# The passes of the feed-forward part on TensorE: copies written out, or a loop

## The chip, the cores and the metric

The kernel runs on one core of a Trainium2 chip. The metric is the device time of one execution in microseconds (us). Three runs of the kernel before are given, and their median counts.

## The reference, cut to what matters

One layer of a decoder trunk, for 512 tokens of width 2048 in float32: a mixer sub-layer and a feed-forward sub-layer, each with a residual. The change lies in the second:

```
hf = modulate(rms_norm(x, norm_ffn_gain), sh_f, sc_f)
gate_h, up_h = split(hf @ w_ffn_in, 2)          # (512, 2048) @ (2048, 11264)
x = x + g_f * ((silu(gate_h) * up_h) @ w_ffn_out)   # (512, 5632) @ (5632, 2048)
```

## The kernel before

Each engine has a program of its own, written out in order in one function, and they meet only at semaphores. The hidden width of 5632 is worked in FG = 11 groups of 512. For each group the two input products (gate and up) are made as two jobs each, a job being a product by a 2 x 2 Winograd scheme: seven block products instead of eight. Every float32 product is made of three passes in a reduced format, high by high, low by high and high by low parts. Two rounds make a job (one for each half of the contraction), so that a group has eight rounds. A round (`wino_round`, lines 1116 to 1141) has seven blocks of 4 x 3 = 12 matmuls of 256 columns. The product with `w_ffn_out` is made by `down_tile`: 16 tiles of 4 x 3 = 12 matmuls of 512 columns in a group.

The rounds overlap the groups: the first eight rounds stand ahead, then come FG - 1 = 10 passes (lines 1162 to 1180), each with rounds 0 and 1 of line 1165, the 16 down tiles of the group before, a matmul without use at line 1175, and rounds 2 to 7. After the passes the last group's down tiles follow.

What the matmuls need is made elsewhere. SyncE loads pairs of weight blocks into the buffer `raw` (line 457), ScalarE writes their high parts `fhi` (lines 1486 and 1496), VectorE makes sums of blocks and most low parts `flo` (lines 2074 to 2092), drains PSUM (lines 2118 to 2126) and adds the down products to the residual (line 2245), GpSimd makes the other low parts (lines 616 and 626). These four already run the passes as hardware loops: lines 486, 630, 1561 and 2249 are `with <engine>.Fori(0, ...) as j`. TensorE's passes are a Python loop that writes out ten copies.

Before each block TensorE waits for its low part, `low_pool` or `low_dve`; before each down tile for `low_pool` and `y_added` (lines 1169 and 1170), before the first also for `drained` and `h_lo` (line 1172); before some rounds for `drained` (line 1144) or `y_added` (line 1125). In a pass these are 97 waits. The values waited for come from the class `Round`, whose methods return a constant when j is a Python number and an expression of a register when j is a loop variable:

```
def ahead(self, n, per):
    return n if self.j is None else per * self.j + n
def blocks(self, n):
    return self.ahead(self.block + n, 72)
def lows(self, n):
    return self.ahead(self.low + n, 32)
def owns(self, n):
    return self.ahead(self.own + n, 40)
```

The buffers and PSUM banks that a pass uses do not depend on j: a pass moves the ring of six blocks by 72 and the buffer of eight by 48 places.

Of the kernel before, what the change touches and what calls it, by code (L numbers as in the profile page):

```python
# [20 lines left out]
FG = FFN // (4 * P)  # L21
# [51 lines left out]
def layer_kernel(nc, xt, wstream, mstream, vecs, rows, tabs, cmp_tab, up, pool_w, w1, w2, out):  # L73
    with ExitStack() as ctx:
# [568 lines left out]
        def _(pe):  # L643
# [472 lines left out]
            def wino_round(at, job, half, slot, entry=False, banks=None):  # L1116

                for i in range(7):
                    s = at.ring(i)
                    if i in POOL_LOWS:  # L1120
                        pe.wait_ge(low_pool, at.lows(POOL_LOWS.index(i) + 1))
                    else:
                        pe.wait_ge(low_dve, at.owns(DVE_LOWS.index(i) + 1))
                    if banks is not None and i in banks:
                        pe.wait_ge(*banks[i])
                    c = COMBO[i]
                    if entry and 2 <= i < 6:
                        pe.wait_ge(t_low, 4 * half + i - 1)
                    if entry and i == 6:
                        pe.wait_ge(b_low, 8 * (half + 1))  # L1130
                    bank, side = PLACE[i]
                    acc = ps[:, 4 * slot + bank, side * HALF:(side + 1) * HALF]
                    for kp in range(4):
                        if entry and i < 2:
                            pe.wait_ge(b_low, 8 * half + 2 * kp + i + 1)
                        w = slice(kp * P, (kp + 1) * P)
                        for n, (wo, xo) in enumerate(((fhi, hfH), (fhi, hfL), (flo, hfH))):
                            ins = nc.tensor.matmul(acc, wo[:, s, w], xo[half][:, c, kp, :],  # L1138
                                                   start=half == 0 and side == 0 and kp == 0 and n == 0,
                                                   stop=half == 1 and kp == 3 and n == 2, skip_group_check=True)  # L1140
                    ins.then_inc(blk_used, 1)

            def free_slot(job):
                pe.wait_ge(drained, job)

            def down_tile(at, d, bank, kk):
                s = at.ring(d)
                for k in kk:
                    col = slice(k * P, (k + 1) * P)
                    ins = passes(ps[:, bank, :], huH[:, k, :], huL[:, k, :], fhi[:, s, col], flo[:, s, col],  # L1150
                                 False, k == 0, k == 3)
                return ins
# [5 lines left out]
            for x in range(4, 8):  # L1158
                if x % 2 == 0:
                    free_slot(x // 2 - 1)  # L1160
                wino_round(Round(x), x // 2, x % 2, x // 2 % 2)
            for j in range(FG - 1):
                free_slot(4 * j + 3)
                for x in range(2):
                    wino_round(Round(x, j), 0, x, 0)
                at = Down(j)
                pe.wait_ge(drained, 4 * j + 4)
                for d in range(KD):
                    pe.wait_ge(low_pool, at.lows(d + 1))
                    pe.wait_ge(y_added, 16 * j + (d + 1))  # L1170
                    if d == 0:
                        pe.wait_ge(h_lo, 2 * j + 2)
                    down_tile(at, d, 4 + d % 4, range(4)).then_inc(blk_used, 1)
                pe.wait_ge(drained, 4 * j + 5)
                nc.tensor.matmul(ps[:, 1, 0:P], ident[:, :], ones[:, :], start=True, stop=True)
                for x in range(2, 8):
                    if x in (4, 6):
                        free_slot(4 * j + x // 2 + 3)
                    wino_round(Round(x, j), x // 2, x % 2, x // 2 % 2, banks=None if x != 2 else {
                        0: (y_added, 16 * j + 17), 1: (y_added, 16 * j + 18), 2: (y_added, 16 * j + 20)})  # L1180
# [1225 lines left out]
```

## Time and profile before

| | |
|---|---|
| median of three runs | 2467.75 us (2460.15 to 2467.84) |
| profiled execution | 2467.75 us, span 2466.0 us |
| mean granted TensorE clock over the span | 0.972 of 2.4 GHz |
| TensorE busy | 96% of the span, 14,813 matmuls and as many weight loads |
| VectorE, ScalarE, GpSimd busy | 65%, 39%, 41% |
| ten passes | from about 1167 to 2417 us |

In the rows, PE is TensorE's matmuls and PEld its weight loads, DVE is VectorE, ACT ScalarE, POOL GpSimd and SP SyncE; a q behind the name (PEldq) marks what the sequencer handles alone. L1138 is line 1138 of the kernel. The span is the profiled time from the first to the last instruction, and times in the rows count from its start. PEclk is the granted share of 2.4 GHz. EVENT_SEMAPHORE is a separate wait, ALU_OP and FUSED_REGOPS are register operations, COMPARE_BRANCH is a loop's branch. Queues of the kind "instruction" bring program code.

### The profile page before, as it was taken

The numbers are of one execution on the slowest core, as the hardware profiler recorded it, in microseconds if no ns is written. First come the engines' busy times: TensorE is split into PE (matmuls) and PEld (weight loads), VectorE is DVE, ScalarE is ACT, GpSimd is POOL, SyncE is SP. The second block draws the span as 40 slices with busy tenths as digits, with TensorE's granted clock in tenths as the row PEclk, the third lists the DMA queues.
The fourth block names the chain that finished last, engine by engine and source line by source line (L and its number), as shares of the span: only waits on it lengthen the run. The fifth ranks groups of instructions, "written<-read, shape, count | busy, mean of one in ns | idle before, by whom it ended". The sixth has DMA issues, their size and how long they took to land.

```text
span 2466.0 us, 40619 instructions
## 1 busy us (share of the span) xinstructions
PE 2377.2 (96%) x14813; PEld 2121.7 (86%) x14813; DVE 1610.9 (65%) x2449; ACT 971.7 (39%) x1804; POOL 1014.8 (41%) x782
## 2 busy tenths in 40 slices
PE   7989999999799999969999999999999999999999
PEld 5867777877699888859898989898989898999997
DVE  6746335466788577698485858585857575757573
ACT  5343223333566522245343434343434343434332
POOL 5853333446577544312424242424242424242423
PEclk7899999999799999979999999999999999999999
DMA  9842134566112377513333232323232323232323
GB/s 368 284 160 74 60 103 156 185 217 231 47 61 68 129 251 254 196 35 103 103 103 103 103 103 99 107 88 118 86 120 86 120 86 120 86 116 90 111 87 128
DMA packets 86300, 317.16 MB, mean 129 GB/s; under 512 B 9585, under 2 KB 10241, under 8 KB 84737
## 3 DMA queue, kind: packets, MB, share of 16 engines
q1 hardware_dynamic: 84240, 303.31, 36.3%
q10 hardware_dynamic: 1904, 11.62, 1.2%
q8 instruction: 118, 1.93, 0.3%
q14 instruction: 38, 0.30, 0.0%
HBM read 310.69 MB, written 4.19 MB: 128 GB/s over the span
## 4 chain that ended last, share of the span: by engine, by line
PE 75%; issue 11%; DVE 6%; POOL 5%; DMA 1%; ACT 0%; SPq 0%; POOLq 0%; ACTq 0%; DVEq 0%
PE ps L1138 35%; PE ps L647 31%; POOL wlo L513 5%; PE ps L1030 2%; PE ps L1019 1%; PE ps L986 1%; PE ps L987 1%; PE ps L719 1%; DVE macc L1603 1%; DMA modx<-in_mstream 1%; DVE pacc L1628 1%; DVE biasT L1950 0%; PE ps L1085 0%; DVE hf L2159 0%; POOL pacc L534 0%
## 5 line engine op out<-in xcount | busy, mean ns | idle before, releaser
L1138 PE MATMUL ps<-hfH,fhi 128*128 128x256 f32 x2464 | 710.6, 288 | 23.5 <-DVE hfL L2178 7.5
L1138 PE MATMUL ps<-hfH,flo 128*128 128x256 f32 x2464 | 700.9, 284 | 0.0
L1138 PE MATMUL ps<-hfL,fhi 128*128 128x256 f32 x2464 | 693.9, 282 | 0.0
L616 POOL TENSOR_TENSOR flo<-raw,fhi 128x512 fp32r<-128x512 f32 x176 | 241.6, 1373 | 784.2 <-ACT fhi L1486 783.8
L1138 PEld LDWEIGHTS ps<-hfH,fhi 128*128 128x128 f32 x2464 | 466.6, 189 | 26.9 <-issue 12.9
L1138 PEld LDWEIGHTS ps<-hfL,fhi 128*128 128x128 f32 x2464 | 478.6, 194 | 0.0
L1138 PEld LDWEIGHTS ps<-hfH,flo 128*128 128x128 f32 x2464 | 465.0, 189 | 0.0
L1486 ACT ACTIVATE fhi<-fsum 128x512 fp32r<-128x512 f32 x352 | 221.0, 632 | 392.6 <-DVE fsum L2074 130.9
L2092 DVE TENSOR_TENSOR flo<-fsum,fhi 128x512 fp32r<-128x512 f32 x352 | 307.9, 887 | 9.5
L2245 DVE SCALAR_TENSOR_TENSOR x1T<-ps,modc,x1T 128x512 f32<-128x512 f32 x176 | 132.1, 751 | 273.5 <-PE ps L647 270.8
L626 POOL TENSOR_TENSOR flo<-raw,fhi 128x512 fp32r<-128x512 f32 x176 | 234.4, 1345 | 155.6 <-ACT fhi L1496 154.9
L647 PE MATMUL ps<-huH,fhi 128*128 128x512 f32 x704 | 275.8, 392 | 1.2 <-DVE huL L2135 1.2
L647 PE MATMUL ps<-huH,flo 128*128 128x512 f32 x704 | 276.7, 393 | 0.0
L647 PE MATMUL ps<-huL,fhi 128*128 128x512 f32 x704 | 275.7, 392 | 0.0
L513 POOL TENSOR_TENSOR wlo<-raw,whi 128x512 fp32r<-128x512 f32 x112 | 158.5, 1417 | 250.1 <-ACT whi L1277 250.1
L1496 ACT ACTIVATE fhi<-raw 128x512 fp32r<-128x512 f32 x176 | 109.0, 630 | 255.8 <-PE ps L647 206.8
L520 POOL TENSOR_TENSOR wlo<-raw,whi 128x512 fp32r<-128x512 f32 x100 | 144.9, 1459 | 150.0 <-ACT whi L1207 143.7
L1486 ACT ACTIVATE fhi<-raw 128x512 fp32r<-128x512 f32 x264 | 163.4, 624 | 86.0 <-PE ps L647 49.1
L647 PE MATMUL ps<-whi,hmH 128*128 128x512 f32 x448 | 185.4, 414 | 5.5 <-DVE xs L1822 2.9
L1603 DVE SCALAR_TENSOR_TENSOR macc<-modw,cact,macc 128x512 f32<-128x512 f32 x165 | 183.2, 1110 | 7.0 <-DMA modw<-in_mstream 1.4
L1277 ACT ACTIVATE whi<-raw 128x512 fp32r<-128x512 f32 x120 | 75.4, 630 | 264.3 <-PE ps L647 263.7
L647 PE MATMUL ps<-wlo,hmH 128*128 128x512 f32 x448 | 178.7, 399 | 0.0
(321 smaller groups left out, 4226.7 us busy)
## 6 DMA issues: line engine op xcount, KB each, us to landing
raw<-in_wstream SPq DMA_DIRECT2D x370, 512.0 KB, 4.1
modw<-in_mstream SPq DMA_DIRECT2D x144, 512.0 KB, 5.4
modx<-in_mstream SPq DMA_DIRECT2D x32, 512.0 KB, 5.5
modg<-in_mstream SPq DMA_DIRECT2D x16, 512.0 KB, 5.4
xT<-in_xt SPq DMA_DIRECT2D x4, 1024.0 KB, 8.1
w1s<-in_w ACTq DMA_DIRECT2D x2, 2048.0 KB, 8.8
x1T<-in_xt ACTq DMA_DIRECT2D x4, 1024.0 KB, 8.2
out_y<-x1T SPq DMA_DIRECT2D x16, 256.0 KB, 2.0
```

The lines of the kernel that those rows point to most:

```text
L513: nc.gpsimd.tensor_tensor(wlo[:, s, :], raw[:, r, :], whi[:, s, :].bitcast(F32), ALU.subtract).then_inc(unit_ready, 1)
L520: TT(wlo[:, u % SPLIT, :], raw[:, u % 8, :], whi[:, u % SPLIT, :].bitcast(F32), ALU.subtract).then_inc(unit_ready, 1)
L616: TT(flo[:, s, :], src, fhi[:, s, :].bitcast(F32), ALU.subtract).then_inc(low_pool, 1)
L626: TT(flo[:, s, :], raw[:, at.slot(d), :], fhi[:, s, :].bitcast(F32), ALU.subtract).then_inc(low_pool, 1)
L647: ins = nc.tensor.matmul(acc, lhs, rhs, start=first and n == 0, stop=last and n == 2)
L1138: ins = nc.tensor.matmul(acc, wo[:, s, w], xo[half][:, c, kp, :], start=half == 0 and side == 0 and kp == 0 and n == 0, stop=half == 1 and ...
L1277: A(whi[:, u % SPLIT, :], raw[:, u % 8, :], ACT.Copy).then_inc(unit_hi, 1)
L1486: A(fhi[:, at.ring(i), :], src, ACT.Copy).then_inc(blk_hi, 1)
L1496: A(fhi[:, at.ring(d), :], raw[:, at.slot(d), :], ACT.Copy).then_inc(blk_hi, 1)
L1603: ins = V.scalar_tensor_tensor(out=macc[:, :], in0=src, scalar=scal, in1=macc[:, :], op0=ALU.mult, op1=ALU.add)
L2092: V.tensor_tensor(flo[:, s, :], src, fhi[:, s, :].bitcast(F32), ALU.subtract).then_inc(low_dve, 1)
L2245: V.scalar_tensor_tensor(out=x1T[:, d, :], in0=ps[:, bank, :], scalar=modc[:, M_GF + d:M_GF + d + 1], in1=x1T[:, d, :], op0=ALU.mult, op1= ...
```

## The change

TensorE's ten passes become a hardware loop of its own. The body is the same; the values of its waits become expressions of the loop's register. Nothing else is changed, on TensorE or elsewhere.

```
-            for j in range(FG - 1):
+            with pe.Fori(0, FG - 1) as j:
                 free_slot(4 * j + 3)
                 for x in range(2):
                     wino_round(Round(x, j), 0, x, 0)
```

## Rows read from the trace of the kernel before

**Rows 1.** The page: busy time of TensorE, and the chain that ended last.

```profile
PE 2377.2 (96%) x14813; PEld 2121.7 (86%) x14813; DVE 1610.9 (65%) x2449; ACT 971.7 (39%) x1804; POOL 1014.8 (41%) x782
...
PE ps L1138 35%; PE ps L647 31%; POOL wlo L513 5%; PE ps L1030 2%; PE ps L1019 1%; PE ps L986 1%; PE ps L987 1%; PE ps L719 1%; DVE macc L1603 1%; DMA modx<-in_mstream 1%; DVE pacc L1628 1%; DVE biasT L1950 0%; PE ps L1085 0%; DVE hf L2159 0%; POOL pacc L534 0%
```

**Rows 2.** Stretches of 125 us: busy us and count of each engine.

```profile
core 0: us, PE busy (x) PEld busy (x) DVE busy (x) ACT busy (x) POOL busy (x), PEclk, DMA share, GB/s
1231.10:1356.10 125.00, 125.00 (x868) 116.86 (x867) 82.28 (x120) 49.05 (x80) 43.01 (x32) 1.00 0.31 102
...
2231.10:2356.10 125.00, 125.00 (x868) 116.86 (x867) 82.29 (x120) 49.06 (x80) 43.04 (x32) 1.00 0.31 102
```

**Rows 3.** Line 1175: count, duration in ns, first and last start in us.

```profile
L1175 PE MATMUL ps<-ones,ident x20: 270/272/273, 1231.1 to 2356.3; 128*128 128x128 f32 x20
```

**Rows 4.** Instruction queue q8 (packets, MB, share): pass 1481.1 to 1606.1; whole run.

```profile
q8 instruction: 7, 0.11, 0.4%
...
q8 instruction: 118, 1.93, 0.3%
```

**Rows 5.** Register work of the loops on VectorE and ScalarE, ten passes: ns min/median/max.

```profile
L2249 DVEq FUSED_REGOPS  x10: 62/63/63, 1159.8 to 2285.2; - x10
L370 ACTq ALU_OP  x390: 35/35/49, 1159.8 to 2407.3; - x195
L370 DVEq ALU_OP  x170: 40/40/52, 1161.9 to 2407.3; - x170
L2087 DVEq ALU_OP  x390: 40/40/40, 1164.1 to 2409.2; - x195
L2089 DVEq ALU_OP  x160: 40/40/40, 1165.7 to 2408.5; - x160
```

**Rows 6.** Lines 1172 and 647 from 1558 to 1563 us.

```profile
L1172 PEldq EVENT_SEMAPHORE  x1: 51/51/51, 1559.9 to 1559.9; - x1
...
L647 PEld LDWEIGHTS ps<-huH,fhi x2: 187/187/187, 1561.8 to 1562.4; 128*128 128x128 f32 x2
```

**Rows 7.** VectorE's loop, line 2249: a taken branch, then the last.

```profile
L2249 DVEq ALU_OP  x1: 40/40/40, 1409.7 to 1409.7; - x1
L2249 DVEq COMPARE_BRANCH  x1: 67/67/67, 1409.8 to 1409.8; - x1
L2249 DVEq FUSED_REGOPS  x1: 63/63/63, 1410.1 to 1410.1; - x1
...
L2249 DVEq COMPARE_BRANCH  x1: 50/50/50, 2409.9 to 2409.9; - x1
```

**Rows 8.** Instruction queues: 1159 to 1285; 1300 to 2410 (no q14); 2411.1 to 2412.

```profile
q14 instruction: 3, 0.02, 0.1%
...
q8 instruction: 61, 1.00, 0.4%
...
q14 instruction: 1, 0.01, 3.8%
```

**Rows 9.** DMA issues of the run: count, KB each, median us to landing.

```profile
raw<-in_wstream SPq DMA_DIRECT2D x370, 512.0 KB, 4.1
...
ident<-in_tabs SPq DMA_DIRECT2D x1, 64.0 KB, 2.1
```

**Rows 10.** TensorE's waits near 548, 402, 2423 us, and stretches just after them.

```profile
PE ps L647 <- POOL wlo L513: 2.6, 1, 2.6
...
PE ps L647 <- DVE xs L1822: 2.9, 2, 2.1
...
PE ps L647 <- DVE huL L2135: 1.2, 1, 1.2
...
404.20:407.60 3.40, 2.90 (x7) 2.35 (x8) 3.37 (x14) 0.00 (x0) 0.00 (x0) 0.50 0.00 0
...
551.00:554.40 3.40, 3.40 (x9) 2.64 (x8) 3.33 (x3) 0.14 (x1) 3.40 (x3) 0.51 0.36 133
...
2424.00:2431.00 7.00, 7.00 (x31) 5.72 (x32) 3.00 (x4) 2.54 (x4) 4.48 (x4) 1.00 0.14 36
```

More of the change, by code:

```diff
@@ L1161, in _ @@
                 wino_round(Round(x), x // 2, x % 2, x // 2 % 2)
-            for j in range(FG - 1):
+            with pe.Fori(0, FG - 1) as j:
                 free_slot(4 * j + 3)
```

## The prediction

> **What bounds the kernel now.** I read the page first, then the stretches of the feed-forward part, the one instruction that occurs once in a pass, the instruction transfers, and last the loops that other engines already run. The page says that TensorE is busy 96% of the span and heads the chain of work that ended last, with line 1138 (the Winograd rounds) as its largest entry [rows 1]. The stretches say more: between 1231 and 2356 us TensorE is busy 125.00 us of 125.00, at a granted clock of 1.00 (2.4 GHz) in the first pass as in the last, while DVE has 82, ACT 49 and POOL 43 us of work [rows 2]. So in these ten passes TensorE waits for nobody, and every us that it stops is a us on the end. The pass itself: the warming matmul of line 1175 stands once in it (two records each, 0.1 us apart), first at 1231.1 and last at 2356.3 us [rows 3], so one pass takes (2356.3 - 0.1 - 1231.1) / 9 = 125.0 us.
>
> How its code arrives is the second thing to see. In one pass TensorE runs 868 + 867 recorded matmuls and weight loads [rows 2] and some twenty separate waits (1755 instructions), and queue q8 brings 7 instruction packets, 0.11 MB [rows 4]: packets of 16 KB with about 1755 / 7 = 250 instructions each, one every 18 us. Over the run q8 brought 118 packets, 1.93 MB [rows 4]. That is straight code that streams in; none of it stops TensorE today.
>
> **What the change removes and adds.** It removes nine of ten copies of the pass from TensorE's program. The matmuls, weight loads, waits and signals executed are the same in number and order: 84 matmuls in each of eight rounds, 192 in the down tiles, one for warmth. Nothing moves between engines, and no other queue changes. It adds four things.
>
> *Register work for the waits.* A wait for 72j + 56 was a constant and is now computed. The other engines show the price: for DVE one operation of 40 ns before most waits, for ACT 35 ns, and once a pass a fused operation of some 60 ns [rows 5]. TensorE has 97 waits in a pass, of which no two neighbours share a value, so some 97 x 0.04 + 5 x 0.06 = 4.2 us of sequencer work a pass. It lies ahead of the array: the wait of line 1172 (before the first down tile) was dealt with at 1559.9 us, and the first weight load of that tile starts at 1561.8 us [rows 6]. So the sequencer runs 1.9 to 2.0 us ahead (some 17 matmuls of 0.12 us), with one or two register operations per block of 12 matmuls (12 x 0.12 = 1.44 us). Cost 0; if that cover were gone, 4.2 x 10 = 42 us.
>
> *The loop's own instructions.* On DVE the add (40 ns), the compare-and-branch and then the first instruction of the next pass stand at 1409.7, 1409.8 and 1410.1 us [rows 7]: 0.3 us from branch to next instruction, though the target is there. With the first register operations 0.45 us per taken branch. Under a lead of 2.0 us it costs nothing by itself.
>
> *Code that must be there when the branch is taken.* The body is 1755 + about 105 = 1860 instructions, 1860 / 250 = 7.4 packets of 16 KB, so it touches 8 blocks, perhaps 9, and the block after it is fetched ahead. The nearest row is DVE's loop: q14 (8 KB packets) brought 3 in the stretch of its first pass, and from 1300 to 2410 us none at all [rows 8], so its body is kept. But that body is 120 busy instructions [rows 2] and, of three lines alone, (170 + 390 + 160) / 10 = 72 register operations [rows 5]: at some 128 instructions to an 8 KB packet it touches two or three blocks, not eight. No row says that a body of TensorE's length is kept. I take it that the first block has been overwritten when the branch comes, so that it is fetched anew at each of the 9 taken branches.
>
> The price of that fetch, F, has to be bounded. When DVE left its loop (branch at 2409.9 us, rows 7), q14 was empty up to 2411.1 and then had one packet [rows 8]: over 1.2 us from need to start. A 16 KB packet then takes 0.3% of 16 engines' 2466 us over 118 packets, 118 / 118 = 1.0 us [rows 4]. Low end 2.2 us. High end: 4.1 us, the landing of a 512 KB weight transfer among others [rows 9]. Between them: a 64 KB transfer lands in 2.1 us [rows 9], of which a 4 KB share of one engine is a small part; with 1.0 us for the packet 2.9, and some more for the weight loads that keep the queues 30% busy [rows 2]. I take 3.3.
>
> The stall per branch is then 0.45 + 3.3 - 2.0 = 1.75 us (0.65 at the low end, 2.55 at the high), and nine make 16 us.
>
> *The clock.* After a stop the granted clock may fall to half (1.2 GHz). A wait of 2.6 us near 548 us was followed by 3.4 us at 0.51; one of 2.1 us near 402 by 3.4 us at 0.50; one of 1.2 us near 2423 left it at 1.00 [rows 10]. A stop of 1.75 lies between. Where the clock falls, the array does half the work for 3.4 us, so 1.7 us are lost, in nine such places 15 us, or twice that if it stays down twice as long. I take it as kept for the likeliest case.
>
> **A rule against this.** The row above gives a lead of 2.0 us. The Trainium skill, "Advanced Engine Details and Errata", section "Engine Queue Depths", gives TensorE's queue 64 entries. By that, 32 matmuls of 0.12 us, 3.8 us, would be queued when the branch is reached, 0.45 + 3.3 would be covered, and the sum would be 0. The trace's lead speaks against it. The skill's "Runtime: NRT & Kernel Launch", section "Instruction fetch mechanics", speaks both ways: 2048 instructions of room for PE, which would hold 1860, and a fetch stall for a taken branch outside a two-page window. No run here shows either yet.
>
> **Sum.** The profiled execution took 2467.75 us with a span of 2466.0, and is itself the median of the three runs. 2467.75 + 9 x 1.75 = 2483.5 us, +0.6%. A measurement of this kernel tells about 0.3% (7.4 us) from no change.
>
> **Rivals.**
> 1. *The code stays, or the lead covers the fetch* (the side of no change). For it: DVE's, ACT's and POOL's loops run without a fetch, and the body is a sixteenth of the 118 packets. Against it: length, and a measured lead of 2.0 us against a need of at least 2.65. It decides where 0.45 + F falls under 2.0 + 0.8. Time: 2467.75 plus nine branches that cost nothing, 2468 us. Were F at its low end, 9 x 0.65 = 6 us, 2474, still inside 0.3%. Chance 0.28.
> 2. *The clock falls too.* A stop of over 2 us at every back edge, 1.7 to 3.4 us more for each: 9 x (1.75 + 1.7) = 31 to 9 x (2.55 + 3.4) = 54 us, 2499 to 2521. For it: two waits of 2.1 and 2.6 us did it. Against it: the rest of each 125 us is dense. Chance 0.24.
> 3. *Register work comes out into the open*: if a wait on a register value keeps the sequencer from running ahead, up to 42 us, 2510. Against it: no DVE row shows its wait instructions slow. Chance 0.05.
> 4. *Faster.* There is no wait in these passes to take away; only fewer instruction packets (0.4% of the DMA share in a pass). Chance 0.02, some 2460.
>
> **How the numbers follow.** The likeliest (one fetch per branch, clock kept) has 0.41, with its own range 2474 to 2492 (F from 2.2 to 4.1, stops of 0.65 to 2.55: 6 to 23 us). The range has to reach down to rival 1, whose chance is too large to leave out, and up into rival 2: 2465 to 2508, leaving out the upper part of rivals 2 and 3 and most of rival 4. Slower by over 0.3% means over 2475.2: 0.39 of the likeliest, 0.24 and 0.05, together 0.68. Same: 0.28 and 0.02, 0.30. Faster 0.02.
>
> **What would show it.** Right: a gap of 1 to 2.5 us before the first matmul of line 1138 at nine places 126 to 127 us apart, put down to issue and not to a semaphore; q8 with one or two packets a pass; the rest of the pass 125.0 us as before; register operations on the weight loads' sequencer with no gap behind them. Wrong for want of a fetch: no q8 packet in the later passes and no gap. Wrong in size: a stretch at 0.5 clock behind the gaps, or more than one gap a pass. Seven q8 packets a pass would mean that nothing is kept; the sum stays, since blocks further on are fetched ahead.

## The result, and the profile after

The loop is slower. Over four runs each, the median is 2506.65 us (2504.11 to 2509.25) against 2463.95 us for the kernel before: 42.7 us more, a ratio of 1.0175 with a 95% interval of 1.0147 to 1.0202. The forecast was 2483.5 us, 16 us more. The way and the range held, and the size was less than half of what came.

The profile of the changed kernel, first the page, in the lines that answer to [rows 1] and to the whole run in [rows 4]:

```profile
span 2510.2 us, 41370 instructions
...
PE 2389.8 (95%) x14813; PEld 2130.7 (85%) x14813; DVE 1621.4 (65%) x2449; ACT 973.6 (39%) x1804; POOL 1014.4 (40%) x782
...
q8 instruction: 137, 2.24, 0.4%
...
issue 43%; PE 30%; POOL 20%; DVE 7%; DMA 1%; ACT 1%; POOLq 0%; ACTq 0%; DVEq 0%; SPq 0%
```

As many matmuls as before. The chain that ended last runs through "issue" for 43% of the span, where it was 11% in the kernel before; that share is no measure of the loss, since TensorE's stops in the loop add up to 29 of 2510 us (below). The code queue brings 137 packets, more than the 118 of the straight program, though nine of the ten copies of the pass are gone: 9 packets come in each pass.

Next, line 1175, once a pass as in [rows 3], and the loop's own instructions at line 1162 (count, ns min/median/max, first and last start):

```profile
L1175 PE MATMUL ps<-ones,ident x20: 270/272/273, 1233.1 to 2399.3; 128*128 128x128 f32 x20
...
L1162 PEldq FUSED_REGOPS  x10: 50/50/53, 1166.8 to 2332.5; - x10
L1162 PEldq ALU_OP  x10: 32/32/32, 1291.7 to 2456.7; - x10
L1162 PEldq COMPARE_BRANCH  x10: 76/5282/5727, 1291.8 to 2456.8; - x10
```

A pass takes (2399.3 - 0.1 - 1233.1) / 9 = 129.6 us instead of 125.0. The last branch, not taken, takes 76 ns, and a taken one 5.3 us in the median; DVE's took 67 ns and 0.3 us to the next instruction [rows 7]. The stall arises there.

One of the nine branches in order of time: the instruction itself, the matmuls around it, and stretches with the granted clock, as in [rows 2].

```profile
L1162 PEldq COMPARE_BRANCH  x1: 5514/5514/5514, 1549.1 to 1549.1; - x1
L1162 PEldq FUSED_REGOPS  x1: 50/50/50, 1554.6 to 1554.6; - x1
```

```profile
1550.95 0.28 PE L1138 MATMUL ps<-hfH,flo 128*128 128x256 f32 x1
1554.85 0.58 PE L1138 MATMUL ps<-hfH,fhi 128*128 128x256 f32 x1 [3.61 <-issue]
1555.22 0.41 PE L1138 MATMUL ps<-hfL,fhi 128*128 128x256 f32 x1
```

```profile
1549.00:1551.20 2.20, 2.20 (x19) 2.02 (x18) 2.07 (x4) 1.44 (x3) 0.00 (x0) 1.00 0.89 296
1551.20:1554.80 3.60, 0.03 (x1) 0.00 (x0) 0.49 (x1) 1.21 (x3) 1.26 (x1) 0.78 0.29 115
1554.80:1560.00 5.20, 5.15 (x24) 5.16 (x25) 2.16 (x4) 0.63 (x1) 0.00 (x0) 0.50 0.01 3
1560.00:1566.00 6.00, 6.00 (x53) 6.00 (x53) 5.80 (x12) 3.28 (x5) 1.29 (x1) 1.00 0.52 175
```

The branch begins at 1549.1 us. Until 1551.2 the array works off what was queued, 2.1 us, the lead of [rows 6]. Then it stands for 3.6 us, and when it starts again its clock is at 0.50 (1.2 GHz) up to 1560. In those 5.2 us it does half the work, so 2.6 us more are lost.

What TensorE waited for in the loop (total us, times, longest):

```profile
PE ps L1138 <- issue: 18.1, 5, 3.8
PE ps L1138 <- POOL flo L616: 11.1, 4, 3.2
```

### The profile page after: what moved, and what is told of

Same layout as the page of the kernel before. It is cut to its first block, busy times and chain, and to the rows that moved or that the text cites. A ratio compares the mean times of both kernels' runs of the same rounds, so it can differ in the third digit from the quotient of the medians.

```text
span 2510.2 us, 41370 instructions
## 1 busy us (share of the span) xinstructions
PE 2389.8 (95%) x14813; PEld 2130.7 (85%) x14813; DVE 1621.4 (65%) x2449; ACT 973.6 (39%) x1804; POOL 1014.4 (40%) x782
## 4 chain that ended last, share of the span: by engine, by line
issue 43%; PE 30%; POOL 20%; DVE 7%; DMA 1%; ACT 1%; POOLq 0%; ACTq 0%; DVEq 0%; SPq 0%
PE ps L647 15%; POOL flo L616 7%; POOL flo L626 7%; PE ps L1138 6%; POOL wlo L513 5%; PE ps L1030 2%; PE ps L1019 1%; PE ps L986 1%; PE ps L719 1%; PE ps L987 1%; PE ps L740 1%; DVE macc L1603 1%; DVE pacc L1628 1%; DVE biasT L1950 0%; PE ps L1085 0%
## 5 line engine op out<-in xcount | busy, mean ns | idle before, releaser
L1138 PE MATMUL ps<-hfL,fhi 128*128 128x256 f32 x2464 | 702.4, 285 | 0.0
L1138 PEld LDWEIGHTS ps<-hfH,fhi 128*128 128x128 f32 x2464 | 476.5, 193 | 58.1 <-issue 32.1
L1138 PEld LDWEIGHTS ps<-hfH,flo 128*128 128x128 f32 x2464 | 473.9, 192 | 0.0
L2092 DVE TENSOR_TENSOR flo<-fsum,fhi 128x512 fp32r<-128x512 f32 x352 | 321.7, 927 | 10.1
L647 PE MATMUL ps<-whi,hmL 128*128 128x512 f32 x448 | 178.8, 399 | 0.0
```

What stands on the lines that cost most here:

```text
L647: ins = nc.tensor.matmul(acc, lhs, rhs, start=first and n == 0, stop=last and n == 2)
L2092: V.tensor_tensor(flo[:, s, :], src, fhi[:, s, :].bitcast(F32), ALU.subtract).then_inc(low_dve, 1)
```

## The experiments

Each run is compared with runs of the kernel before on the same chip; "loop" is the changed kernel.

**1. The register work alone.** Ten copies as before, with the waits on a register that is counted up between them:

```
-            for j in range(FG - 1):
+            j_reg = pe.alloc_register("pass_j")
+            pe.reg_mov(j_reg, 0)
+            for copy in range(FG - 1):
+                j = pe.snap(j_reg, min_val=0, max_val=FG - 2)
 ...
+                pe.reg_add(j_reg, j_reg, 1)
```

> Ten passes written out, but every wait of a pass is on a register value as in the loop; no branch. Theory (the branch waits for code): the register work hides under the sequencer's lead, 2464 us as the kernel before, within 5, no gap at the pass ends. Rival (register work or waits on register values slow TensorE): 2500 to 2510 us as the loop. Both in part: between, say 2475.

2467.09 us against 2465.56; ratio 1.0007 (0.9992 to 1.0023). TensorE's register operations stand in its trace at 32 ns each, 39 of them a pass for the waits on `low_dve` alone, and it has no gap in the passes:

```profile
L1123 PEldq ALU_OP  x390: 32/32/42, 1166.1 to 2403.9; - x195
...
1290.00:2340.00 1050.00, 1050.00 (x7252) 977.80 (x7252) 694.00 (x1003) 409.90 (x671) 371.80 (x276) 1.00 0.32 103
```

So the register work costs nothing that can be told from zero (-2 to +6 us), and rival 3 falls.

**2. A hint for the branch.** The loop with one instruction more at the top of each pass, a hint for its own branch:

```
-            for j in range(FG - 1):
+            with nc.Fori(0, FG - 1, engines=[mybir.EngineType.PE], hint_back_edge=True) as j:
```

2466.96 us against 2465.56; ratio 1.0004 (0.9987 to 1.0021): the whole 42 us are gone. The branch, and the transfers from 1290 to 2410 us:

```profile
L1162 PEldq COMPARE_BRANCH  x10: 88/228/253, 1290.5 to 2415.6; - x10
```

```profile
q1 hardware_dynamic: 31085, 113.18, 30.4%
issues: line engine op xcount, KB each, median us to landing
```

A taken branch takes 228 ns in the median, and the line of q8 is missing: no code is brought at all in nine passes. So the cost hangs on the missing code. No early fetch of the target is seen either: there is nothing to fetch. In the loop a code packet, that of the next block, starts 1.5 to 2.0 us before every branch; here there is none in the 16 us before the first one (1274.6 to 1290.4 us):

```profile
q1 hardware_dynamic: 320, 1.18, 24.9%
q14 instruction: 1, 0.01, 0.2%
```

That fits the last line of the expectation, that the hint keeps the next block out and the body stays; how it does so is not shown.

**3. Fewer branches.** Two passes in the body, five times:

```
-            for j in range(FG - 1):
+            def one_pass(j):
 ...
+            with pe.Fori(0, (FG - 1) // 2) as half:
+                one_pass(2 * half)
+                one_pass(2 * half + 1)
```

> The loop's body holds two passes, so 4 branches are taken instead of 9; register work as in the loop. Theory: 4/9 of 43 us, 2483 us (2478 to 2490), each branch again 4.4 to 5.7 us. Rival (register work): 2506 us. Rival (cost grows with the length of the body): also near 2506.

2479.36 us against 2465.56; ratio 1.0064 (1.0043 to 1.0084), 13.8 us (11 to 21) for four taken branches of 4.3 to 5.4 us. It goes with the number of branches and not with the length of the body. In the profile the four stops are 11.9 us and the clock fell behind two of them only, those of 3.5 us; behind the stops of 2.4 and 2.6 us it stayed at 1.00. That gives less than the 19 us expected.

**4. The same loop cut in the down tiles.** The body begins with down tile 8 of a pass and ends with tile 7 of the next:

```
-            for j in range(FG - 1):
 ...
+            head(0, 8)
+            with pe.Fori(0, FG - 2) as j:
+                tail(j, 8)
+                head(j + 1, 8)
+            tail(FG - 2, 8)
```

> The same loop cut at another place: the back edge stands between the down tiles 7 and 8, 8 branches are taken. The sequencer's lead of 17 matmuls is 17 x 0.23 = 3.9 us there instead of 17 x 0.12 = 2.0. Theory: branch of 5.3 us as before, gap 5.3 + 0.1 - 3.9 = 1.5 us, clock mostly kept: 8 x 1.5 = 12, 2476 us (2470 to 2484). Rival (the lead does not cover the fetch, or cost lies elsewhere): 8/9 x 43 = 38, 2502 us.

2466.27 us against 2465.56; ratio 1.0001 (0.9981 to 1.002): better than I expected. The branches (line 1189), and the matmuls at the end of one of them:

```profile
L1189 PEldq COMPARE_BRANCH  x9: 83/3667/3926, 1330.9 to 2325.7; - x9
```

```profile
1459.08 0.39 PE L647 MATMUL ps<-huL,fhi 128*128 128x512 f32 x1
1459.30 0.40 PE L647 MATMUL ps<-huH,flo 128*128 128x512 f32 x1
1459.54 0.39 PE L647 MATMUL ps<-huH,fhi 128*128 128x512 f32 x1
```

The branch ended at 1459.5 us, and there is no gap: 17 matmuls of 512 columns start behind the branch's start and before the first of the new pass, and 17 x 0.23 = 3.9 us. That lead is shown to cover a branch of this length. But the branch is also shorter here, 3.3 to 3.9 us instead of 4.4 to 5.7, which my theory did not have.

**5. A body that fits, and the same body placed so that it does not.** The three kernels leave out the third product (high parts of the hidden values by low parts of the weights) in the down tiles of the ten passes, so a pass has 1702 instructions in the loop. One is written out, one is a loop that begins on a block of 256 instructions, one begins 160 into a block:

```
+            with nc.Fori(0, FG - 1, engines=[mybir.EngineType.PE], head_slot={mybir.EngineType.PE: 0}) as j:
 ...
-                    down_tile(at, d, 4 + d % 4, range(4)).then_inc(blk_used, 1)
+                    down_tile(at, d, 4 + d % 4, range(4), short=True).then_inc(blk_used, 1)
```

> Ten passes written out as before, but their down tiles leave out the third product (high parts of the hidden values by low parts of the weights): 64 of 866 matmuls less in a pass, so the output is less exact. It is the base for the two short loops: 125.0 - 64 x 0.23 = 110.3 us a pass, 2464 - 147 = 2317 us if TensorE stays the bound; if another chain takes over, more.

2325.32 us (2316.16 to 2328.43), 8 more than expected. In its profile, the shortest of the four runs, a pass takes 109.5 us.

> The loop over the shortened pass (third product of the down tiles left out; 1830 - 128 = 1702 instructions), placed so that it begins on a block of 256: 7 blocks and the one ahead, 8. Theory (room for 8 blocks, the one fetched ahead included): no instruction packet in the later passes, branch under 0.5 us, the time of the same work written out (2317 us). Rival (a body of this length is never kept, or any taken branch of TensorE costs 5 us): 9 x 3 to 9 x 5 us more, 2345 to 2360, with 8 packets a pass.

2329.21 us (2321.59 to 2338.14).

> The very same instructions as the other short loop, but beginning 160 into a block, so that they touch 8 blocks, and with the one ahead 9. Theory: nothing is kept, 9 instruction packets a pass, and each branch waits again. The last block was entered 70 instructions before the branch (4.2 us), so no other fetch is in the way: branch 3.3 to 3.9 us, gap 1.4 to 1.9, 9 x 1.7 = 15 us over the other short loop, some more where the clock falls. Rival (only the length counts, not the place): no difference between the two.

2364.11 us (2359.99 to 2368.07). The code transfers from 1280 us to the end of the loop, first of the loop at 0, then of the one at 160, and their branches:

```profile
q1 hardware_dynamic: 30970, 112.74, 34.9%
issues: line engine op xcount, KB each, median us to landing
```

```profile
q1 hardware_dynamic: 31002, 112.85, 33.9%
q8 instruction: 80, 1.31, 0.5%
```

```profile
L1167 PEldq COMPARE_BRANCH  x11: 76/208/4492, 1162.9 to 2268.7; - x11
```

```profile
L1167 PEldq COMPARE_BRANCH  x11: 76/4698/5758, 1168.3 to 2314.4; - x11
```

The same instructions in another place cost 35 us. In the first, whose blocks are 7 and the one ahead 8, the back edges (the loop's taken branches) take 0.2 us and nothing is fetched (the 4.5 us are the one jump over the padding on the way in, which stopped TensorE for 2.6 us). The 3.9 us between this loop and the written-out passes are inside the spread of their runs. In the second, 8 blocks and the one ahead, each pass fetches 9 packets (80 in nearly nine passes): not the one block that had to give way, but all. So the room is for eight blocks of 16 KB, the one ahead counted in. The Trainium skill, "Runtime: NRT & Kernel Launch", section "Instruction fetch mechanics", gives PE 128 KiB and these runs agree; its two-page window, for a taken branch, they do not bear out. The time of the second was missed (35 us over the first instead of some 15): its branches took 4.4 to 5.8 us, not the 3.3 to 3.9 expected.

**6. Is it the fetch of the next block that is in the way?** The full loop, begun 96 into a block, with `head_slot` 96 and nothing else:

> The full loop, with its body begun 96 into a block, so that its end lies 96 + 1830 - 7 x 256 = 134 instructions (8 us) behind the last crossing, instead of just behind it. Theory (in the changed kernel the branch has to let the fetch of the block ahead end first, which began 1.5 to 2 us earlier, and then pays its own 3.4 us): branch 3.3 to 3.9 us instead of 4.4 to 5.7, gap 1.4 to 1.9 instead of 2.4 to 3.8, clock mostly kept, 9 x 1.7 = 15, 2480 us (2476 to 2490). Rival (5.3 us is simply the price of the fetch): 2506 us.

2509.17 us against 2461.42; ratio 1.0187 (1.0161 to 1.0212). The branches (line 1162) are as long as ever:

```profile
L1162 PEldq COMPARE_BRANCH  x11: 76/5439/5778, 1167.5 to 2454.8; - x11
```

The forecast of 2480 us fails: the last code packet before each branch was now 7.3 to 7.5 us back, and the branch waited all the same. What the trace does show is the other queue. DMA in the first 3.2 us of the loop's branch at 1549.1, and in the 1.1 us after that:

```profile
q1 hardware_dynamic: 274, 1.02, 90.1%
...
q1 hardware_dynamic: 14, 0.02, 5.9%
q8 instruction: 1, 0.02, 5.5%
```

Two weight transfers, 1.02 MB, keep the 16 engines 90% busy, and the code packet starts when they are nearly done. They are the two that SyncE issues at the end of a pass (lines 488 to 490). In the cut of experiment 4 the weights come after the code packet.

The nine passes of the loop differ in when these two are issued. Their issue before the branch of 5.5 us at 1549.1, then before another branch, with that branch:

```profile
L457 SPq DMA_DIRECT2D raw<-in_wstream x2: 333/404/475, 1548.1 to 1548.7; - x2
...
L457 SPq DMA_DIRECT2D raw<-in_wstream x2: 333/568/804, 1937.7 to 1938.3; - x2
L1162 PEldq COMPARE_BRANCH  x1: 4629/4629/4629, 1939.7 to 1939.7; - x1
```

In six passes the first is issued 1.0 us before the branch, and the branch takes 5.1 to 5.7 us; in three, 1.8 to 2.0 us before it, and the branch takes 4.4 to 4.7.

**7. The transfers held back.** SyncE issues these two only when TensorE has used the last block of the pass, in the loop and, as a control, in the kernel before:

```
                 for p in range(4):
                     free_round(Round(6 + p // 2, j), p % 2)
+                    if p == 2:
+                        sp.wait_ge(blk_used, 72 * j + 128)
                     load_next(24 + p, j)
```

> The full loop, and SyncE holds back the two weight transfers (512 KB each) that it issues at the end of a pass until TensorE has used the pass's last block (about 2 us after the branch begins). Theory (the code fetch stands behind these transfers): its packet starts 1.0 to 1.6 us behind the branch instead of 2.0 to 3.4, branch 3.3 to 3.9 us instead of 4.4 to 5.7, gap 1.4 to 1.8 instead of 2.4 to 3.8, clock mostly kept: 9 x 1.6 = 14, 2478 us (2474 to 2488). Rival (the transfers only happen to be there): 2506 us, branch 5.3 us.

2477.99 us against 2468.09; ratio 1.0051 (1.0031 to 1.007).

> The same holding back of the two transfers in the kernel before, with its ten copies. It is the control: the weights are wanted some 10 us later, so nothing, 2464 us within 5. If the transfers come too late, TensorE waits at each pass and the other run must be read against this one.

2465.77 us; ratio 0.9998 (0.9982 to 1.0015). The loop's branches (line 1164), its waits, and the DMA in the first 0.9 us of the branch at 1791.6, the 2.5 us after that, and the 4 us in which the transfers now come:

```profile
L1164 PEldq COMPARE_BRANCH  x10: 76/3470/3841, 1284.2 to 2419.6; - x10
```

```profile
PE ps L1140 <- issue: 15.2, 9, 2.0
```

```profile
DMA packets 0, 0.00 MB, mean 0 GB/s; under 512 B 0, under 2 KB 0, under 8 KB 0
...
q1 hardware_dynamic: 8, 0.03, 12.8%
q8 instruction: 1, 0.02, 2.3%
...
q1 hardware_dynamic: 226, 0.86, 63.3%
```

With the DMA engines idle the branch takes 3.4 to 3.8 us, the stops are 15.2 us instead of 29.2, and the clock fell behind two of them instead of nine. The fetch of the next block still starts 1.4 to 1.9 us before each branch here, so it is not what made the branch of the loop long; experiment 6, whose weights came as close to the branch as before, could not tell that by itself. Most of the loss, 42.7 us in the loop and 9.9 here, is gone by moving two transfers that have nothing to do with the loop.

**8. A stop of the sequencer without any missing code.** The kernel before, with signals and waits of its own at nine pass ends, 64 or 20 of them:

```
+                if j:
+                    for n in range(64):
+                        pe.sem_inc(spare, 1)
+                        pe.wait_ge(spare, 64 * (j - 1) + n + 1)
```

> The kernel before with its ten copies, and at nine pass ends 64 signals and waits of TensorE's own sequencer in a row, instead of a branch: it stands for S = 64 x 0.05 to 64 x 0.1 = 3.3 to 6.4 us, and no code is missing. Theory (what counts is how long the sequencer stands, less its lead of 2.0 us, and the clock after that): gap S - 2.0, and for S near 5.3 the same 42 us as the loop, 2506; in general 9 x (S - 2.0) plus 1.5 to 3 us for each half-clock stretch. Rival (much of the 42 us comes from the fetched body or the weight path): clearly less than the loop at the same S.

2547.32 us against 2468.09; ratio 1.0333 (1.0307 to 1.0359).

> The same with 20 signals and waits: S = 1.0 to 2.0 us, under the lead of 2.0. Theory: no gap, 2464 us within 5. Rival (the lead does not cover a stop of the sequencer): 9 x S = 9 to 18 us, 2473 to 2482.

2470.62 us; ratio 1.0011 (0.9995 to 1.0027). A pair takes 0.15 us, more than I had bounded, so both stops are longer than planned. The start of the first and the last of one series of 64, and of one of 20, and TensorE's waits:

```profile
L1166 PEldq EVENT_SEMAPHORE  x64: 51/51/51, 1420.8 to 1430.7; - x64
```

```profile
PE ps L1139 <- PEq L1166: 69.0, 9, 7.8
```

```profile
L1166 PEldq EVENT_SEMAPHORE  x20: 51/51/51, 1416.0 to 1419.0; - x20
```

```profile
PE ps L1139 <- PEq L1166: 7.9, 9, 0.9
```

The series of 64 last 9.6 to 9.9 us and gave stops of 69.0 / 9 = 7.7 us, those of 20 last 2.95 us and gave 0.9: in both, the stop is the standing less 2.1 us. Nine stops of 0.9 left the clock at full, and the expected "no gap" did not come. So a sequencer that stands longer than its lead stops TensorE with all its code there too. The comparison with the loop at the same length of standing was not made, as the long series came out nearly twice as long as the loop's branch. The sums agree in kind: 69 us of stops and 20 us for work at half clock stand against 79 us measured, in the loop 29 and 21 against 43. Both sums are too large, by 7 to 10 us. That 7.9 us of short stops moved the median by only 2.5 (-1 to 7) is the same surplus; the last section has what is known of it.

## Why the prediction was right or wrong

**TensorE is the bound and each of its stops counts**: right. Its passes had no wait before, and 29.2 us of stops came out at the end.

**Register work under the lead, cost 0**: right (experiment 1). **A lead of 2.0 us**: right (2.1 in experiment 8), and in the down tiles 3.9 us (experiment 4). The queue of 64 entries of the Trainium skill ("Advanced Engine Details and Errata", section "Engine Queue Depths"), which stood against it, is not borne out: 17 matmuls and their weight loads are 34.

**The code is fetched anew at each of nine branches**: right. The length counted in blocks with the one ahead is the reason (experiments 2 and 5), but that the room ends below it I had only assumed; no row showed it, and at one block less the guess would have been wrong. Of q8 I had expected one or two packets a pass as the first sign; it was the sign of "nothing is kept", nine where I had said seven. As I had said, that leaves the sum, because the blocks further on are fetched ahead.

**The price of that fetch is the step that failed**, and with it the clock, which I had put at nothing. I took F = 3.3 us, and with the rest 0.45 + 3.3 - 2.0 = 1.75 us a stop, 16 us in all. With idle DMA engines the term is right: branches of 3.4 to 3.8 us and stops of 1.5 to 2.0 (experiment 7), and 3.3 to 3.9 us a branch in experiment 4. In the loop as changed the code packet stands behind 1 MB of weights that SyncE issues 1 to 2 us before the branch; the branch takes 4.4 to 5.7 us, and the stops are 29 us in all, eight of the nine above the 2.55 us that I had drawn as the high end. I had written "some more for the weight loads" from their mean share of 30%. The mean was the wrong number: from the branch to the start of its code packet, 2.0 to 3.4 us, the share is some 90% in every pass. In the program the last low parts of a pass release the transfers, and TensorE's last blocks need the same parts just ahead of the branch. The trace of before had it: around 1539.8 us, where the branch of that pass would stand (58.7 us behind line 1175, as in the loop), the two were issued at 1537.7 and 1538.3 us, and from 1538.8 to 1541.8 the queues had

```profile
q1 hardware_dynamic: 262, 0.99, 83.7%
```

**The clock kept**: wrong, in large part as a consequence. Stops of 1.5 to 2.0 us left it up in seven of nine cases (experiment 7), and the loop's stops of 2.4 to 3.8 brought it down in nine of nine, each time for 3.4 or 6.8 us. Read from the stretches at half rate that the array worked in, that is 1.7 us behind the three shorter stops and 2.5 to 2.8 behind the six longer, 21 us together: more than the 13 us or so by which the stops themselves were undersized. The length of the stop alone does not decide it. The clock stayed at 1.00 behind stops of 2.4 and 2.6 us in experiment 3, of 2.5 and 2.8 in the loop at 160 of experiment 5, and of 3.3 in experiment 6 (its stop, and the stretch after it):

```profile
PE ps L1138 <- issue: 3.3, 1, 3.3
...
1296.70:1303.00 6.30, 6.30 (x53) 6.30 (x54) 4.49 (x10) 1.90 (x3) 1.30 (x1) 1.00 0.18 46
```

What else decides was not found. So rival 2 was what happened, by its own mechanism: 29 for the stops and 21 for the clock, less some 9 that the passes took less for themselves, make the 41 us by which the nine passes of the profile grew (129.6 - 125.0 = 4.6 each). The sign "the rest of the pass 125.0 us as before" was wrong by that: in seven of the nine it was 123.4 to 123.7. This surplus also flatters experiment 7, whose 15.2 us of stops and 3.4 for the clock came out as 9.9. In the prediction's own sums the upper end of the likeliest case is 2467.75 + 23 = 2491, not 2492, which changes nothing.

**Rival 1** (no change) would have needed the code to stay, which experiment 5 shows for a body one block shorter, or the lead to cover it, which experiment 4 shows for another place in the pass. **Rival 3** fell in experiment 1.

No version was shown to beat the kernel before. The hinted loop and the one cut in the down tiles equal it, with a tenth of the code for the passes.

## What to carry to other kernels

Count a loop's body in fetch blocks, and add the one ahead: TensorE had room for eight blocks of 256 instructions with that one, and one more made it fetch all nine in each pass. A branch to missing code took 3.3 to 3.9 us, or up to 5.8 when a weight transfer was in the queues just then; look at the DMA share at the branch and not at its mean. Two things took the whole cost away: a back edge among the 512-column matmuls, where the sequencer's lead of 17 matmuls lasts 3.9 us instead of 2.0 and no transfer stood in the way, and a hint, with which nothing was fetched.

## What the runs showed of the hardware that was not expected

A full branch miss has three parts. In experiment 7, 1.0 to 1.3 us passed to the start of the packet, 0.9 to 1.3 us it took, and 1.4 us passed to the end of the branch. The last part is the same in all loops (1.35 to 1.54 us).

The passes have two rhythms at the same granted clock. In the trace of experiment 1 (the matmul that stands once a pass, line 1178, two neighbouring passes early and late):

```profile
L1178 PE MATMUL ps<-ones,ident x4: 271/272/273, 1353.1 to 1477.0; 128*128 128x128 f32 x4
...
L1178 PE MATMUL ps<-ones,ident x4: 271/272/274, 2096.8 to 2221.9; 128*128 128x128 f32 x4
```

A pass takes 123.8 us early and 125.0 late, with no wait in either and the clock at 1.00; all nine passes of the kernel before took 125.0 in its profile. A pass behind a stop was mostly in the shorter rhythm (in the loop seven of nine, in experiment 7 seven of nine), which gives back part of what the stop cost. Nine times 1.2 us is 11 us, half the spread of the kernel before from run to run (2452 to 2474 us in all). What sets the rhythm was not tried and is left open.
